# The experts' gate and up projections in f16 halves with a power of two per expert, in a decoder layer with 32 experts

## The chip, the cores and the metric

One core of one Trainium2 chip runs the whole layer in one launch. The metric is the device time of that launch in microseconds, smaller is better. TensorE (PE) multiplies, VectorE (DVE) and ScalarE (ACT) do elementwise work, GpSimd (POOL) gathers and scatters rows, SyncE (SP) issues the large loads. "Block" below means 128 rows of tokens that belong to one expert.

## What is computed

```python
h <- h + W_out[ norm(attention(n(h))) ++ norm(conv(n(h))) ]   # "mixer", 4096 tokens, width 1024
h <- h + HierMoE(n(h))                                        # top-1 group of 4, then top-2 of its 8 experts

def expert_block(args):          # tokens sorted by expert, blocks of 128 rows
    xb, e = args                 # xb 128 x 1024, w_g[e] and w_u[e] 1024 x 512, w_d[e] 512 x 1024
    return (jax.nn.silu(xb @ w_g[e]) * (xb @ w_u[e])) @ w_d[e]
y = ybuf[dest] * gate_s          # weighted by the router's gate and summed per token
```

All inputs are f32. The products have to be nearly f32 exact, so each operand is split into a high and a low half and three products are summed: hi·hi, hi·lo and lo·hi.

## The kernel before

**Two stages.** `mixer` (L211) computes attention, convolution, output projection and routing for 32 tiles of 128 tokens; its projections multiply f16 halves (L574). It ends by writing for every expert a list of its tokens, and a table `blocks_of` with each expert's number of blocks and its first block (L1507 to L1520). `experts` (L1535) then walks through the experts and their blocks; each engine runs its own copy of that walk (`walk`, L1564), and the engines meet in semaphores only.

**One block on PE** (`block_`, L1704): 24 matmuls of 512 columns into psA (gate: 8 slices of the contraction, 3 products each), 4 transposes of the previous block's activation into psE (`turn_act`), 24 matmuls into psB (up), 8 transposes of the next block's gathered rows into psC and psD (`transpose_rows`), and 24 matmuls into psF and psG that are the down projection of the previous block. All these operands (`gT_hi`, `gT_lo`, `aT_hi`, `aT_lo` and the weights' halves) are in the 4-byte format float32r.

**The weights of an expert**: three loads of 2 MB each by SP into the raw buffers `raw["gate"]`, `raw["up"]`, `raw["down"]`, one buffer each (`load_expert`, L168; issued in `sync`, L1587, in the fixed order gate, up, down). SP issues the next expert's load as soon as the present one has been split: ACT copies 512 columns at a time into `hi` (L1770), DVE subtracts that from the raw weights into `lo` (L1812), eight slices each. There is one set of halves, so the split of a new expert begins when the last block of the old one no longer needs them (`gate_ps`, `up_ps`, `y_ps`); PE waits slice by slice (L1673).

**ACT's order in a block** (`halves`, L1734, with L1772 to L1797): in an expert's first block the gate split, `copy_y` (result rows out of psF), in the first block the up split, `turn` (psE into `aT_hi`), `silu` (psA into `gated`), `turn_x` (psC and psD into `gT_hi` for the next block, L1796), and in the first block the down split. DVE follows the same order with the low halves, the product of up and gated (L1826) and its half of the rows (L1819). PE's next block begins when both halves of `gT` are there.

**POOL** loads a block's list of tokens (`slots`, L1632), gathers its rows (L1600), copies row numbers (L1609) and scatters finished rows with an add (L1612).

Of the kernel before, what the change touches and what calls it, by code (L numbers as in the profile page):

```python
# [24 lines left out]
ALU = mybir.AluOpType  # L25
# [9 lines left out]
P = 128  # L35
# [103 lines left out]
def build(nc, x, meta_tokens, rel_bias, mix_norm_g, w_in, q_norm_g, k_norm_g, attn_sinks, conv_w,  # L139
# [12 lines left out]
    with ExitStack() as keep:  # L152
# [24 lines left out]
        rows_of_y = ksb("rows_of_y", [P, 1], I32)  # L177

# [32 lines left out]
def mixer(nc, ctx, env):  # L211
# [3 lines left out]
     cst, ident, blocks_of, held, wi_all, load_expert, raw, keep) = (env[n] for n in (  # L215
         "x2 meta_tokens rel_bias mix_norm_g w_in q_norm_g k_norm_g attn_sinks conv_w attn_out_norm_g "
         "conv_out_norm_g w_out ffn_norm_g w_group_router b_group_router w_expert_router b_expert_router "
         "consts onehot out table hn_dram u_dram band_dram bcast cst ident blocks_of held wi_all load_expert raw keep").split())
# [14 lines left out]
    rt_stat = sb("rt_stat", [P, 8])  # L233
# [71 lines left out]
    hn_scale, inv_rt = rt_stat[:, 4:5], rt_stat[:, 7:8]  # L305
# [58 lines left out]
    planned = 18  # L364
# [711 lines left out]
    def vector(dve):  # L1076
# [60 lines left out]
        def scales_of_router():  # L1137
# [19 lines left out]
            set_up(v.tensor_scalar(inv_rt.bitcast(I32), sI[:, 3:4], float(-(9 << 23)), None, ALU.add))  # L1157
            set_up(v.tensor_scalar(inv_rt, inv_rt, rt_stat[:, 6:7], None, ALU.mult))
# [351 lines left out]
        step(v.tensor_scalar(blocks_of[:, counts], blocks_of[:, E:], 1, None, ALU.max))  # L1510
        step(v.tensor_scalar(blocks_of[:, 0:1], blocks_of[:, 0:1], 2, None, ALU.max))
# [23 lines left out]
def experts(nc, ctx, env):  # L1535
    out, table, hn_dram, cst, ident, blocks_of, held, raw, raw_in, load_expert, keep, mixed = (env[n] for n in (
        "out table hn_dram cst ident blocks_of held raw raw_in load_expert keep mixed").split())
    slots, slots_old, rows_of_y = (env[n] for n in ("slots", "slots_old", "rows_of_y"))
# [8 lines left out]
    hi = {n: sb(f"{n}_hi", [P, 8, 512], F32R) for n in raw}  # L1547
    lo = {n: sb(f"{n}_lo", [P, 8, 512], F32R) for n in raw}
# [4 lines left out]
    y = sb("y", [P, D])  # L1553

    hi_s = {n: sem(f"hi_s_{n}") for n in raw}
    lo_s = {n: sem(f"lo_s_{n}") for n in raw}
    slots_in, moved, shifted, rows_in = sem("slots_in"), sem("moved"), sem("shifted"), sem("rows_in")
# [4 lines left out]
    named = sem("named")  # L1562

    def walk(eng, block, before=None):  # L1564


        def loads(e):
            n = eng.value_load(blocks_of[0:1, bass.ds(e, 1)], min_val=1, max_val=TILES)
            base = eng.value_load(blocks_of[0:1, bass.ds(e + E, 1)], min_val=0, max_val=3 * TILES)
            return n, base  # L1570

        n, _ = loads(0)
        block(0, 0, 0, True)
        block(0, 1, 1, False)
        with eng.If(n > 2):
            with eng.Fori(2, n) as i:
                block(0, i, i, False)
        with eng.Fori(1, E) as e:
            n, base = loads(e)
            block(e, 0, base, True)  # L1580
            with eng.If(n > 1):
                with eng.Fori(1, n) as i:
                    block(e, i, base + i, False)
        n, base = loads(E - 1)
        return base + n

    def sync(sp):  # L1587
        mixed(sp)

        with sp.Fori(1, E) as e:  # L1590
            for n in raw:
                sp.wait_ge(hi_s[n], 8 * e)
                sp.wait_ge(lo_s[n], 8 * e)
                load_expert(sp, n, e)

    def gpsimd(pool):
# [27 lines left out]
        def block_(e, i, b, first):  # L1624
# [13 lines left out]
            if known:  # L1638
# [8 lines left out]
            if known and b == 1:  # L1647
                pool.wait_ge(added, 32)


# [17 lines left out]
    def tensor(pe):  # L1668
        def split_mm(ps, l_k, left, right, r_k, fresh, name=None, e=0):

            for n, k in enumerate(l_k):
                if fresh:
                    pe.wait_ge(hi_s[name], e * 8 + r_k[n] + 1)  # L1673
                    pe.wait_ge(lo_s[name], e * 8 + r_k[n] + 1)
# [19 lines left out]
        def down(b):  # L1694
# [5 lines left out]
            for half, ps in enumerate((psF, psG)):  # L1700
                split_mm(ps, range(KE), (aT_hi, aT_lo), (hi["down"], lo["down"]), [2 * k + half for k in range(KE)],
                         False).then_inc(y_ps, 1)
# [170 lines left out]
```

## Time and profile before

| | us |
|---|---|
| median of 3 runs | 2752.85 (2752.47 to 2755.39) |
| the profiled execution | 2750.93 |
| its span in the trace | 2749.3 |
| mixer and hand-over, up to the first expert matmul | 1329.8 |
| experts, from there to the end | 1419.5 |
| PE busy | 2643.6 (96% of the span) |
| DVE busy, ACT busy | 1716.2, 1391.3 |
| mean granted clock of TensorE | 0.987 of 2.4 GHz |

A time at the start of a row is measured from the start of the span. The profiled execution has 1.6 us outside its span. Durations are per instruction; on PE, ACT and DVE the next instruction starts a little before the former one's duration is over, so the distance of starts is shorter than the duration.

### The profile page before, as it was taken

The numbers are of one execution on the slowest core, as the hardware profiler recorded it, in microseconds if no ns is written. First come the engines' busy times: TensorE is split into PE (matmuls) and PEld (weight loads), VectorE is DVE, ScalarE is ACT, GpSimd is POOL, SyncE is SP. The second block draws the span as 40 slices with busy tenths as digits, with TensorE's granted clock in tenths as the row PEclk, the third lists the DMA queues.
The fourth block names the chain that finished last, engine by engine and source line by source line (L and its number), as shares of the span: only waits on it lengthen the run. The fifth ranks groups of instructions, "written<-read, shape, count | busy, mean of one in ns | idle before, by whom it ended". The sixth has DMA issues, their size and how long they took to land.

```text
span 2749.3 us, 49924 instructions
## 1 busy us (share of the span) xinstructions
PE 2643.6 (96%) x14252; PEld 1820.9 (66%) x14253; DVE 1716.2 (62%) x3920; ACT 1391.3 (51%) x3046; POOL 798.8 (29%) x825
## 2 busy tenths in 40 slices
PE   4999999999999999996699999999999999999997
PEld 2455555555555555553588888888888888888886
DVE  5677777777777777776454455545655444546633
ACT  7666555565555566553344445445545333435533
POOL 1122323232322222331232333323223323333232
PEclk9999999999999999998799999999999999999999
DMA  8376555556655555656556677667767665667763
GB/s 315 82 166 166 156 160 158 152 157 165 163 152 160 154 156 164 166 138 167 187 169 189 186 236 244 200 196 224 235 186 232 205 183 153 194 180 237 235 181 54
DMA packets 546395, 495.22 MB, mean 180 GB/s; under 512 B 411787, under 2 KB 411948, under 8 KB 545340
## 3 DMA queue, kind: packets, MB, share of 16 engines
q1 hardware_dynamic: 517516, 406.08, 49.2%
q0 software_dynamic: 28848, 88.77, 13.8%
q8 instruction: 14, 0.23, 0.0%
q14 instruction: 17, 0.14, 0.0%
HBM read 309.74 MB, written 87.88 MB: 145 GB/s over the span
## 4 chain that ended last, share of the span: by engine, by line
PE 89%; DVE 3%; DMA 3%; ACT 2%; issue 1%; SPq 1%; POOL 1%; POOLq 0%; DVEq 0%; ACTq 0%
PE psB L1676 15%; PE psA L1676 15%; PE psG L574 11%; PE psF L1676 7%; PE psG L1676 7%; PE psE L574 6%; PE psF L574 6%; PE psD L574 6%; PE psC L574 6%; PE psH L574 3%; PE psC L1684 1%; PE psD L1684 1%; PE psE L1691 1%; DMA xg<-hn_rows,slots 1%; DMA slots<-slot_table 1%
## 5 line engine op out<-in xcount | busy, mean ns | idle before, releaser
L574 PE MATMUL psG<-wi_all,both_xT 128*128 128x512 f16 x1536 | 345.2, 382 | 10.9 <-DMA both_xT<-x 10.9
L574 PEld LDWEIGHTS psG<-wi_all,both_xT 128*128 128x128 f16 x1536 | 148.7, 98 | 188.2 <-DMA both_xT<-x 11.1
L1600 POOL DMA_INDIRECT xg<-hn_rows,slots x80 | 99.2, 1240 | 544.0 <-DMA slots<-slot_table 389.4
L1676 PE MATMUL psB<-up_hi,gT_hi 128*128 128x512 f32 x632 | 254.4, 402 | 0.0
L1676 PE MATMUL psA<-gate_hi,gT_hi 128*128 128x512 f32 x632 | 247.3, 391 | 3.1 <-ACT gT_hi L1796 1.7
L1812 DVE TENSOR_TENSOR down_lo<-wi_all,down_hi 128x512 fp32r<-128x512 f32 x256 | 157.0, 686 | 147.1 <-ACT down_hi L1770 147.1
L1676 PE MATMUL psB<-up_hi,gT_lo 128*128 128x512 f32 x632 | 247.6, 392 | 0.0
L1676 PE MATMUL psA<-gate_hi,gT_lo 128*128 128x512 f32 x632 | 247.3, 391 | 0.0
L1676 PE MATMUL psA<-gate_lo,gT_hi 128*128 128x512 f32 x632 | 247.0, 391 | 0.0
L1676 PE MATMUL psB<-up_lo,gT_hi 128*128 128x512 f32 x632 | 246.4, 390 | 0.0
L1796 ACT ACTIVATE gT_hi<-psC 128x512 fp32r<-128x512 f32 x80 | 47.8, 597 | 384.8 <-PE psC L1684 384.8
L1826 DVE TENSOR_TENSOR act_rows<-psB,gated 128x512 f32<-128x512 f32 x79 | 54.6, 691 | 289.6 <-PE psB L1676 289.6
L1770 ACT ACTIVATE down_hi<-wi_all 128x512 fp32r<-128x512 f32 x256 | 137.0, 618 | 149.1 <-PE psG L1676 149.1
L819 ACT ACTIVATE prob<-prob,soft,s_stat 128x256 f32<-128x256 f32 x256 | 150.6, 589 | 94.2 <-DVE soft L1206 94.1
L1609 POOL COPY rows_of_y<-slots 128x1 int32<-128x1 int32 x80 | 129.3, 1616 | 236.9 <-DVE y L1819 236.2
L1812 DVE TENSOR_TENSOR gate_lo<-wi_all,gate_hi 128x512 fp32r<-128x512 f32 x256 | 157.0, 686 | 46.2 <-ACT gate_hi L1770 46.2
L574 PE MATMUL psE<-wo_all,both_mT 128*128 128x512 f16 x768 | 178.5, 383 | 5.9 <-DMA both_mT<-prob 5.9
L574 PE MATMUL psC<-wi_all,both_xT 128*128 128x512 f16 x792 | 178.6, 381 | 4.5 <-DVE wi_all L1186 4.5
L574 PE MATMUL psD<-wi_all,both_xT 128*128 128x512 f16 x792 | 178.2, 380 | 0.0
L574 PE MATMUL psF<-wo_all,both_mT 128*128 128x512 f16 x768 | 176.2, 379 | 0.0
L1770 ACT ACTIVATE gate_hi<-wi_all 128x512 fp32r<-128x512 f32 x256 | 137.0, 618 | 44.5 <-issue 44.5
L1812 DVE TENSOR_TENSOR up_lo<-wi_all,up_hi 128x512 fp32r<-128x512 f32 x256 | 156.7, 685 | 1.0 <-ACT up_hi L1770 1.0
(320 smaller groups left out, 5777.2 us busy)
## 6 DMA issues: line engine op xcount, KB each, us to landing
wi_all<-in_w_gate SPq DMA_DIRECT2D x32, 2048.0 KB, 9.5
wi_all<-in_w_up SPq DMA_DIRECT2D x32, 2048.0 KB, 12.9
wi_all<-in_w_down SPq DMA_DIRECT2D x32, 2048.0 KB, 11.7
xt<-in_x SPq DMA_DIRECT2D x32, 512.0 KB, 3.7
um<-u_rows SPq DMA_DIRECT2D x64, 256.0 KB, 2.7
out_rows<-h SPq DMA_DIRECT2D x32, 512.0 KB, 3.0
xres<-in_x SPq DMA_DIRECT2D x31, 512.0 KB, 4.1
hn_rows<-xres SPq DMA_DIRECT2D x31, 512.0 KB, 2.9
```

The costliest lines, as they stand in the source:

```text
L574: m = nc.tensor.matmul(ps, left[:, l, k, :], weights.half(r, k, n, width), start=(k == opens and j == 0), stop=(k == closes and j == 2))
L819: s.activation(prob[:, hd, :], prob[:, hd, :], ACT.Exp, bias=ntop[:, hd:hd + 1], scale=inv_s, accum_out=psum_[:, hd:hd + 1]).then_inc(p_sb ...
L1600: pool.indirect_dma_start(xg[:], None, hn_dram, bass.IndirectOffsetOnAxis(ap=slots[:, 0, 0:1], axis=0), bounds_check=SEQ + P - 1).then_inc ...
L1609: g.tensor_copy(rows_of_y[:], slots[:, 3, 0:1]).then_inc(named, 1)
L1676: m = nc.tensor.matmul(ps[:, :], l[:, k, :], r[:, r_k[n], :], start=(n == 0 and j == 0), stop=(n == len(l_k) - 1 and j == 2))
L1684: m = nc.tensor.transpose(ps[:, c * P:(c + 1) * P], xg[:, (4 * h + c) * P:(4 * h + c + 1) * P], ident)
L1691: m = nc.tensor.transpose(psE[:, c * P:(c + 1) * P], act_rows[:, c * P:(c + 1) * P], ident)
L1770: s.activation(hi[n][:, k, :], raw[n][:, k, :], ACT.Copy).then_inc(hi_s[n], 1)
L1796: s.activation(gT_hi[:, 4 * h:4 * h + 4, :].rearrange("p k c -> p (k c)"), ps[:, :], ACT.Copy).then_inc(xgT_hi, 1)
L1812: v.tensor_tensor(lo[n][:, k, :], raw[n][:, k, :], hi[n][:, k, :].bitcast(F32), ALU.subtract).then_inc(lo_s[n], 1)
L1826: v.tensor_tensor(act_rows[:], psB[:, :], gated[:], ALU.mult).then_inc(act_s, 1)
```

## The change

Gate and up are split into f16 halves instead of float32r ones. f16 has a short range of exponents, so each expert's gate and up weights are first multiplied by a power of two. To find it, ACT sums the absolute values of the raw weights over each partition (`ACT.Abs` over 4096 columns with `accum_out`), POOL takes the maximum over the partitions (`partition_all_reduce`), and DVE makes the power and its inverse in five small steps (`scales`). The inverses go into `silu`'s scale and into the product. The rows (`gT`) are scaled by the power `hn_scale` that the router has used already. Down keeps its format and its one set. The halves of gate and up exist twice (`p` is 0 or 1): an expert's gate and up are summed in the first block of the expert before it and split in the second. So each expert takes at least two blocks, and the walk handles the experts in pairs. A split is two chunks of 2048 columns instead of eight of 512.

```diff
-        step(v.tensor_scalar(blocks_of[:, counts], blocks_of[:, E:], 1, None, ALU.max))
-        step(v.tensor_scalar(blocks_of[:, 0:1], blocks_of[:, 0:1], 2, None, ALU.max))
+        step(v.tensor_scalar(blocks_of[:, counts], blocks_of[:, E:], 2, None, ALU.max))
...
-    hi = {n: sb(f"{n}_hi", [P, 8, 512], F32R) for n in raw}
+    hi = {n: [sb(f"{n}_hi_{p}", [P, 8, 512], F16) for p in range(2)] for n in SCALED}
+    hi["down"], lo["down"] = ([sb(f"down_{w}", [P, 8, 512], F32R)] * 2 for w in ("hi", "lo"))
-    gT_hi, gT_lo = sb("gT_hi", [P, KD, P], F32R), sb("gT_lo", [P, KD, P], F32R)
+    gT_hi, gT_lo = sb("gT_hi", [P, KD, P], F16), sb("gT_lo", [P, KD, P], F16)
...
         with sp.Fori(1, E) as e:
             for n in raw:
-                sp.wait_ge(hi_s[n], 8 * e)
-                sp.wait_ge(lo_s[n], 8 * e)
+                sp.wait_ge(hi_s[n], CHUNKS * e)
+                sp.wait_ge(lo_s[n], CHUNKS * e)
                 load_expert(sp, n, e)
...
+        def bound_of(e, p):
+            pool.wait_ge(summed, 2 * (e + 1))
+            hold(pool, held)
+            pool.partition_all_reduce(most(p), sums(p), P, RMAX).then_inc(most_s, 1)
...
+        def sum_up(n, e, p, junk):
             act.wait_ge(raw_in[n], 16 * (e + 1))
+            s.activation(junk, raw[n].rearrange("p k n -> p (k n)"), ACT.Abs, accum_out=sums(p, n)).then_inc(summed, 1)
...
+        def block_(e, i, b, p, last):                                  # on ACT
+            if not (known and b < 2):
+                copy_y(b)
+            if first and not last:
+                sum_next("gate", e, p, b)
+            if not (known and b == 0):
+                turn(b)
+            silu(b, p)
+            if first and not last:
+                sum_next("up", e, p, b)
+            if second and not last:
+                split("gate", e + 1, 1 - p)
+            turn_x(b + 1)
+            if first:
+                split_down(e, b)
+            if second and not last:
+                split("up", e + 1, 1 - p)
```

**ACT, the first block of an expert.** Before, from the loop over the experts (`gate_hi`, `up_hi`, `down_hi` are the splits, `y` is `copy_y`, `gT_hi` is `turn_x`):

```order
L1770 ACTIVATE gate_hi<-wi_all 128x512 [waits raw_in_gate]
L1770 ACTIVATE gate_hi<-wi_all 128x512 x7
...
L1777 ACTIVATE y<-psF,slots 128x512 [waits added]
L1770 ACTIVATE up_hi<-wi_all 128x512 [waits raw_in_up,up_ps]
L1770 ACTIVATE up_hi<-wi_all 128x512 x7
...
L1789 ACTIVATE aT_hi<-psE 128x512 [waits y_ps]
...
L1783 ACTIVATE gated<-psA 128x512 [waits act_s,gate_ps]
...
L1796 ACTIVATE gT_hi<-psC 128x512 [waits xgT_ps]
...
L1796 ACTIVATE gT_hi<-psD 128x512 [waits xgT_ps]
...
L1770 ACTIVATE down_hi<-wi_all 128x512 [waits raw_in_down,y_ps]
L1770 ACTIVATE down_hi<-wi_all 128x512 x7
```

Now, where `gate_hi,own` and `up_hi,own` are the sums of the next expert's raw weights:

```order
L1797 ACTIVATE y<-psF,slots 128x512 [waits added]
...
L1771 ACTIVATE gate_hi,own<-wi_all 128x4096 [waits raw_in_gate]
...
L1809 ACTIVATE aT_hi<-psE 128x512 [waits y_ps]
...
L1803 ACTIVATE gated<-psA,own 128x512 [waits act_s,gate_ps]
L1771 ACTIVATE up_hi,own<-wi_all 128x4096 [waits raw_in_up,up_ps]
...
L1816 ACTIVATE gT_hi<-psC,rt_stat 128x512 [waits xgT_ps]
...
L1816 ACTIVATE gT_hi<-psD,rt_stat 128x512 [waits xgT_ps]
...
L1790 ACTIVATE down_hi<-wi_all 128x2048 [waits y_ps]
L1790 ACTIVATE down_hi<-wi_all 128x2048
```

The splits of gate and up have left this block, and two instructions that wait for the next expert's loads stand ahead of `gT_hi`.

**DVE, the second block of an expert, now** (with the down split's low halves ahead of it, which are issued in the first block):

```order
L1885 TENSOR_TENSOR down_lo<-wi_all,down_hi 128x2048 [waits hi_s_down] x2
...
L1892 TENSOR_SCALAR y<-psG,slots 128x512 [waits added]
...
L1868 TENSOR_SCALAR own<-own 128x2 [waits most_s]
...
L1872 TENSOR_SCALAR own<-own,rt_stat 128x2 [waits step_s]
...
L1904 TENSOR_TENSOR aT_lo<-psE,aT_hi 128x512 [waits step_s,aT_hi_s]
...
L1879 SCALAR_TENSOR_TENSOR gate_lo<-wi_all,own,gate_hi 128x2048 [waits hi_s_gate]
...
L1879 SCALAR_TENSOR_TENSOR gate_lo<-wi_all,own,gate_hi 128x2048 [waits hi_s_gate]
L1900 SCALAR_TENSOR_TENSOR act_rows<-psB,own,gated 128x512 [waits aT_ps,up_ps,silu_s]
...
L1911 SCALAR_TENSOR_TENSOR gT_lo<-psC,rt_stat,gT_hi 128x512 [waits xgT_hi]
...
L1911 SCALAR_TENSOR_TENSOR gT_lo<-psD,rt_stat,gT_hi 128x512 [waits xgT_hi]
L1879 SCALAR_TENSOR_TENSOR up_lo<-wi_all,own,up_hi 128x2048 [waits hi_s_up] x2
```

The low halves of the next expert's gate and up come after the whole of the present expert's down split, and only when the last `up_lo` is done is the raw buffer of up free for another load. SP's own order (gate, up, down) is unchanged.

## Rows read from the trace of the kernel before

**Rows 1.** The page: the chain that ended last, by engine.

```profile
PE 89%; DVE 3%; DMA 3%; ACT 2%; issue 1%; SPq 1%; POOL 1%; POOLq 0%; DVEq 0%; ACTq 0%
```

**Rows 2.** The chain of waits through one block: start us, us, what.

```profile
1434.76 5.44 PE psA L1676 x24
1440.20 0.44 PE psE L1691 x4
1440.64 5.49 PE psB L1676 x24
...
1452.46 5.44 PE psA L1676 x24
```

**Rows 3.** Groups by line on PE, experts: shapes, count | busy us, mean ns.

```profile
L1676 PE MATMUL psA<-gate_hi,gT_hi 128*128 128x512 f32 x632 | 247.3, 391 | 3.1 <-ACT gT_hi L1796 1.7 <-DVE gT_lo L1836 1.5
```

**Rows 4.** The chain of waits in the mixer: f16 matmuls of 512 columns.

```profile
1207.71 5.18 PE psD L574 x24
```

**Rows 5.** Timeline of SP's queue: start us, us, engine, line, what.

```profile
1437.40 0.37 SPq L172 DMA_DIRECT2D wi_all<-in_w_gate  x1
...
1490.52 0.37 SPq L172 DMA_DIRECT2D wi_all<-in_w_gate  x1
...
1525.94 0.37 SPq L172 DMA_DIRECT2D wi_all<-in_w_gate  x1
```

**Rows 6.** ACT by form: scaled and long activations, accumulator read; busy us, mean ns.

```profile
L861 ACT ACTIVATE a<-xres,rt_stat 128x1024 f16<-128x1024 f32 x29 | 33.3, 1148 | 42.1 <-DVE xres L1288 42.1
L803 ACT ACTIVATE wi_all<-wi_all,g_mix 128x1280 f16<-128x1280 f32 x8 | 10.9, 1362 | 5.2 <-DVE wi_all L1186 2.7 <-DVE g_mix L1176 2.5
L791 ACT ACTIVATE wi_all<-wi_all 128x2304 bf16<-128x2304 f32 x8 | 17.0, 2122 | 4.7 <-DMA wi_all<-in_w_in 4.7
L773 ACT ACTIVATION_READ_ACCUMULATOR x<-xt 128x1 f32 x33 | 6.2, 187 | 0.0
```

**Rows 7.** DVE by form: two widths of the instruction that makes f16 halves; `copy_y`.

```profile
L1186 DVE SCALAR_TENSOR_TENSOR wi_all<-wi_all,g_mix 128x1024 f16<-128x1024 f32 x8 | 10.2, 1279 | 0.0
L1186 DVE SCALAR_TENSOR_TENSOR wi_all<-wi_all,g_mix 128x1280 f16<-128x1280 f32 x8 | 12.4, 1552 | 3.1 <-ACT wi_all L803 3.1
L1819 DVE TENSOR_SCALAR y<-psG,slots 128x512 f32<-128x512 f32 x79 | 58.9, 746 | 76.5 <-PE psG L1676 41.7 <-DMA out_rows<-y,rows_of_y 34.8
```

**Rows 8.** Timeline of DVE: two small steps, one waiting for the other.

```profile
1310.69 0.18 DVE L1509 TENSOR_SCALAR blocks_of<-blocks_of 128x32 int32<-128x32 int32 x1
1310.91 0.18 DVE L1510 TENSOR_SCALAR blocks_of<-blocks_of 128x32 int32<-128x32 int32 x1
```

**Rows 9.** Timelines of ACT, DVE and PE at the first expert block.

```profile
1328.40 0.60 ACT L1796 ACTIVATE gT_hi<-psD 128x512 fp32r<-128x512 f32 x1 [0.26 <-PE psD L1684]
1329.03 0.69 DVE L1836 TENSOR_TENSOR gT_lo<-psD,gT_hi 128x512 fp32r<-128x512 f32 x1 [0.16 <-ACT gT_hi L1796]
1329.82 0.77 PE L1676 MATMUL psA<-gate_hi,gT_hi 128*128 128x512 f32 x1 [1.46 <-DVE gT_lo L1836]
```

**Rows 10.** Landing of the 32 up loads (view of the tensor in_w_up).

```profile
DMA to landing us min/median/max: 9.9/12.9/14.0
```

**Rows 11.** POOL by line: the maximum over the partitions.

```profile
L1004 POOL PARTITION_ALL_REDUCE scale_w<-scale_w x2 | 0.7, 365 | 29.7 <-DVE scale_w L1169 29.7
```

**Rows 12.** The chain of waits at the first two expert blocks.

```profile
1329.82 8.12 PE psA L1676 x24
1345.94 5.73 PE psA L1676 x24
```

**Rows 13.** Timeline of PE around a gap in the mixer.

```profile
1275.64 5.04 PE L574 MATMUL psE<-wo_all,both_mT 128*128 128x512 f16 x12 [5.86 <-DMA both_mT<-prob]
1280.52 2.75 PE L574 MATMUL psF<-wo_all,both_mT 128*128 128x512 f16 x12
```

**Rows 14.** Windows in two gaps of PE; last three columns: granted clock, DMA share, GB/s.

```profile
1274.00:1275.60 1.60, 0.00 (x0) 0.00 (x0) 1.06 (x2) 1.57 (x3) 0.00 (x0) 0.50 0.43 108
1289.00:1294.00 5.00, 0.00 (x0) 0.00 (x0) 1.94 (x3) 2.79 (x5) 0.00 (x0) 1.00 0.41 167
1295.00:1299.00 4.00, 0.00 (x0) 0.00 (x0) 3.41 (x18) 0.39 (x2) 0.00 (x0) 0.50 0.78 186
```

**Rows 15.** POOL's copy of row numbers behind a series of splits on DVE (timeline).

```profile
1438.14 4.55 POOL L1609 COPY rows_of_y<-slots 128x1 int32<-128x1 int32 x1 [6.86 <-DVE y L1819]
```

More of the change, by code:

```diff
@@ L363, in mixer @@
     last = sig("last").sem
-    planned = 18
+    planned = 17
     LAST = TILES
@@ L1562, in experts, with walk, expert @@
     named = sem("named")
[L1564 to L1585, printed above, removed]
+    SCALE_STEPS = 5
+    def walk(eng, block):
+        def expert(e, p, last=False):
+            n = eng.value_load(blocks_of[0:1, bass.ds(e, 1)], min_val=2, max_val=TILES)
+            base = eng.value_load(blocks_of[0:1, bass.ds(e + E, 1)], min_val=0, max_val=4 * TILES)
+            start = 0 if isinstance(e, int) and e == 0 else base
+            block(e, 0, start, p, last)
+            block(e, 1, start + 1, p, last)
+            with eng.If(n > 2):
+                with eng.Fori(2, n) as i:
+                    block(e, i, start + i, p, last)
+            return base + n
+        expert(0, 0)
+        with eng.Fori(0, (E - 2) // 2) as pair:
+            expert(pair * 2 + 1, 1)
+            expert(pair * 2 + 2, 0)
+        return expert(E - 1, 1, True)
     def sync(sp):
@@ L1637, in block_ @@
             gather()
-            if known:
+            if known and b < 2:
                 pool.wait_ge(cleared, 3)
@@ L1648, in block_ @@
                 pool.wait_ge(added, 32)
+            if isinstance(i, int) and i == 1 and not last:
+                bound_of(e + 1, 1 - p)
+        bound_of(0, 0)
         mixed(pool)
@@ L1700, in down, with weights, block_ @@
             for half, ps in enumerate((psF, psG)):
-                split_mm(ps, range(KE), (aT_hi, aT_lo), (hi["down"], lo["down"]), [2 * k + half for k in range(KE)],
-                         False).then_inc(y_ps, 1)
-        def block_(e, i, b, first):
+                split_mm(ps, range(KE), (aT_hi, aT_lo), (hi["down"][0], lo["down"][0]),
+                         [2 * k + half for k in range(KE)]).then_inc(y_ps, 1)
+        def weights(n, e):
+            pe.wait_ge(hi_s[n], CHUNKS * (e + 1))
+            pe.wait_ge(lo_s[n], CHUNKS * (e + 1))
+        def block_(e, i, b, p, last):
             static0 = isinstance(b, int) and b == 0
+            first, second = isinstance(i, int) and i == 0, isinstance(i, int) and i == 1
             pe.wait_ge(xgT_hi, 2 * (b + 1))
@@ L1782, in silu @@
                 act.wait_ge(act_s, b)
-            s.activation(gated[:], psA[:, :], ACT.Silu).then_inc(silu_s, 1)
+            s.activation(gated[:], psA[:, :], ACT.Silu, scale=inverse(p, "gate")).then_inc(silu_s, 1)
         def turn(b):
@@ L1845, in vector @@
         dve.sem_inc(y_dve, 3)
-        halves(dve, split, copy_y, product, turn, turn_x)
+        split("gate", 0, 0)
+        turn_x(0)
+        split("up", 0, 0)
+        total = walk(dve, block_)
+        copy_y(total)
+        turn(total)
+        copy_y(total + 1)
     return dict(sync=sync, tensor=tensor, scalar=scalar, gpsimd=gpsimd, vector=vector)
```

175 lines of the change are left out of this document (112 added, 63 removed).

## The prediction, made before the changed kernel was run

> **What bounds the kernel now.** I read the page's chain that ended last first, then the chain of waits in the expert stage, then the timelines of the engines that feed PE. The chain is PE for 89% [rows 1]. In the expert stage one block follows another with no gap: 24 gate matmuls take 5.44 us, 24 up matmuls 5.49, and the next block begins 17.70 us after the last (1452.46 - 1434.76) [rows 2]. The group of one of the three gate products counts 632 matmuls; at 8 a block that is 79 blocks [rows 3]. An expert's length is the distance of two gate loads on SP's queue: 53.12 us is three blocks, 35.42 is two [rows 5]. Of the 30 distances that the trace has, 16 are of two blocks (35.1 to 35.9) and 14 of three; none is of one, so raising the smallest count to two adds no block. The 16 lie in 6 runs of neighbours. So anything that shortens a matmul shortens the kernel, and any lateness of what PE waits for, `gT_hi` and `gT_lo` above all, lengthens it.
>
> **Faster matmuls.** 24 f16 matmuls of 512 columns take 5.18 us in the mixer [rows 4], against 5.44 and 5.49 here [rows 2]. I take 5.18 for gate and 5.23 for up, which starts behind transposes as now: 0.26 twice, 0.52 us a block, times 79 = **-41 us**. The bounds are nothing (the step to f16 brings no pace) and this.
>
> **The new wait.** What the order of ACT shows is that in an expert's first block two sums stand ahead of `gT_hi`, and each waits for a load of the next expert. The load of up cannot be issued before the split of up into the other set is over, a block earlier, because raw weights have one buffer. I follow one turn for a run of two-block experts, with time 0 at the start of the gate matmuls of a second block.
>
> - ACT is free 0.9 us before that: `gT_hi` starts 1.42 before PE does and holds ACT for 0.5 [rows 9]. It splits down in chunks of 2048 columns. 1148 ns at 1024 columns and 1362 at 1280 make 0.84 ns a column, so 2.0 us, or 1.9 from start to start [rows 6]. First chunk done at 1.0.
> - DVE's chunk: 1279 and 1552 ns make 1.07 ns a column, 2.37 us at 2048, 2.3 from start to start [rows 7]. Two chunks of down: 5.6. `copy_y` 0.7 [rows 7]: 6.3. Five steps of `scales`, 0.22 each with its wait [rows 8], and a little for the extra semaphore counts: 7.6.
> - ACT's first chunk of gate: 9.5. DVE's two: 14.1. Product and `gT_lo`: 16.0. Two chunks of up: 20.6. SP then issues the load of up, at 21.0.
> - It lands 9.9 to 14.0 us later, 12.9 in the median [rows 10]. I take 12.9, since a load of gate and a scatter run ahead of and beside it as now: 33.9.
> - The sum: 2122 ns at 2304 columns and 0.84 ns for each of 1792 more, and 187 for the accumulator [rows 6], 3.8 us: 37.7. Then both `gT_hi` and the last `gT_lo`, 0.5 and 1.4 [rows 9]: PE can go on at 39.6.
>
> PE's own work up to there is two blocks, 2 x 17.18 = 34.4. It waits **5.2 us**. In the first expert of a run the block before was on time; then the split of down starts with the end of PE's down matmuls at 0, not at -0.9, and the wait is 6.1. An expert of three blocks gives the chain 17.2 us more and no wait follows. So 10 x 5.2 + 6 x 6.1 = **+89 us**. With a landing of 9.9 the waits are 2.2 and 3.1, together 41; with 14.0 they are 6.3 and 7.2, together 106.
>
> Part of the wait will show one stage earlier: the sum of gate, whose load lands late as well, stands ahead of `aT_hi`, so the down matmuls of the first block will begin a microsecond or two late. This is inside the 5.2, not beside it.
>
> **The start.** Expert 0's up split starts on ACT at about 1329.0 [rows 9]; 1.9 and 4.6 later its raw buffer is free, the load is issued at 1335.9 and, with nothing beside it, lands in 9.9: 1345.8. Plus 3.8 and 1.9 is 1351.5. Block 1 begins at 1345.94 now [rows 12]: **+6 us**. The first sums, of expert 0, lie in the idle time at the end of the mixer.
>
> **The clock.** A gap of 5.86 us in the mixer ended with the granted clock at 0.50, which is 1.2 GHz, and 12 matmuls then took 5.04 us where the next 12 started 2.59 apart in sum (2.75 long) [rows 13, 14]. In another gap the clock was still 1.00 five microseconds in, and 0.50 after six [rows 14]. The new gaps are of this size, partly cut in two. One drop costs about 2.4 us; but the chain above is not PE's, so in a run PE's slowness mostly shortens the next wait. I take a drop in a third of the 17 gaps, half of it felt: with the start's, **+5 us**. Bounds: 0 and 17 x 2.4 = 41. The Trainium skill ("TensorE: Matmul & The Clock Gate", "Why this matters for your kernels") says that pauses between bursts of matmuls let the clock fall back each time. By that rule taken whole the sum would be at the upper bound. The trace agrees for the 5.86 us gap, and shows one gap that held full clock for five.
>
> **At no cost.** The maximum over partitions is 0.4 us [rows 11] and is asked for some 8 us before DVE uses it. But POOL stands in that wait until 37.7, and behind it are the list and the rows of the second block; a fetch and a gather need some 7 us, the transposes come 11.3 after 39.6, so 4 to 5 us of cover are left. If the fetch lies behind a scatter, the cover goes and up to 3 us a wait are added. POOL's small copies can be held up by DVE's splits (4.55 us once per expert now [rows 15]); chunks leave this as it is. Fewer instructions on ACT and DVE save nothing, since neither was waited for. The extra copy and the one step less in the mixer's tail cancel.
>
> **Sum**: -41 + 89 + 6 + 5 = +59. The profiled execution is 2750.9, so 2810; the median of the runs is 1.9 higher, so **2812 us**.
>
> **Rivals.**
> - *The waits are hidden.* If the chain from one second block to the next takes less than 34.4 us, nothing is left but the shorter matmuls: 2752.85 - 41 = 2712 us. For it: two sets of halves, and splits that begin a block ahead. Against it: up would have to land within 7.7 us of its issue, below the fastest of 32. This is the faster side. 0.06.
> - *Loads land early.* With the load of up alone in the queue it may take 9.9: 41 + 6 - 41 = +6, so 2759, and 2770 if waits lie between. 0.12.
> - *The clock falls in every gap.* The sum with 41 in place of 5: 2848. By the skill's rule above this would be the likeliest; the held gap speaks against it, and that a slow PE eats its own wait. 0.14.
> - *f16 brings no pace to PE* (the change does not do what it is for): the wait falls to 4.2 each, since a block stays at 17.70: 73 + 6 + 5 = 2837. Against it: the mixer's f16 matmuls run at 5.18 in the same program. 0.04.
> - The forecast as worked out: 0.60. The rest, 0.04, is a mix of several or a cost unseen.
>
> **Range.** The forecast's own range follows from the landing, 10.5 to 14 us, and the clock: 2775 to 2845. Early loads and the clock rival are taken in down to 2772 and up to 2850. About 0.2% is what a measurement of this kernel can tell from no change, 5.5 us; faster by more 0.07, within 0.05, slower by more 0.88.
>
> **What would show it right.** The 24 gate matmuls at 5.18 us. ACT idle before the Abs on raw up, released by the DMA of up, and PE idle before psA of an expert's second block for about 5 us, released by `gT_hi` or `gT_lo`, 16 or 17 times; no such idle time after an expert of three blocks. SP's up load some 6.4 us behind gate's, and gate loads of a two-block expert about 39.6 us apart. It is wrong if PE's idle time lies elsewhere (POOL's rows, the weights' own waits), if PE has no idle time, or if matmuls keep 5.44.

## The result, and the profile after

The changed kernel takes 2846.3 us, the median of 4 runs (2842.2 to 2849.9), against 2753.1 us (2752.5 to 2755.4): a ratio of 1.034, 95% interval 1.032 to 1.036. The forecast was 2812, with a range of 2772 to 2850. So the sign and the range held, the range by 4 us, and 34 us were missing from the sum.

| | before | after |
|---|---|---|
| span of the profiled execution | 2749.3 us | 2843.3 us |
| mean granted clock | 0.987 | 0.974 |
| first gate matmul of the experts | 1329.82 | 1335.17 |
| second block begins | 1345.94 | 1357.12 |
| block with no wait in it | 17.70 us | 17.16 us |

The page of the kernel after, busy time by engine, and the chain that ended last:

```profile
PE 2635.8 (93%) x14252; PEld 1485.7 (52%) x14253; DVE 1725.0 (61%) x3504; ACT 1597.3 (56%) x2598; POOL 722.7 (25%) x857
...
PE 73%; DMA 12%; issue 5%; DVE 4%; ACT 3%; SPq 1%; POOL 1%; POOLq 1%; DVEq 0%; ACTq 0%
```

PE had 89% of the chain [rows 1] and now has 73%; DMA went from 3% to 12%. What took PE's place is seen in the chain of waits around the first long wait of the experts (start us, us, what):

```profile
1546.05 2.73 PE psG L1703 x12
1548.78 0.03 issue
...
1551.48 0.19 ACT up_hi L1771
1551.66 1.16 ACT gT_hi L1816 x2
1552.83 1.07 issue
1553.90 7.25 PE psA L1703 x24
1561.15 0.44 PE psE L1718 x4
```

PE is done with an expert's first block at 1548.78 and cannot go on until ACT has read out the sum of up (the row of 0.19) and made `gT_hi`. The gap is 5.1 us. The chain calls the last 1.07 us "issue"; the timeline shows what they are, the low halves of the rows on DVE:

```profile
1553.06 0.74 DVE L1911 SCALAR_TENSOR_TENSOR gT_lo<-psD,rt_stat,gT_hi 128x512 f16<-128x512 f32 x1
1553.90 0.59 PE L1703 MATMUL psA<-gate_hi,gT_hi 128*128 128x512 f16 x1 [5.13 <-issue]
```

The 24 gate matmuls behind the gap take 7.25 us, not 5.18. The windows before the gap, in it and over these matmuls show the clock (the last three columns are granted clock, DMA share, GB/s):

```profile
1531.40:1548.70 17.30, 17.25 (x84) 10.43 (x84) 6.37 (x5) 6.19 (x6) 3.67 (x3) 1.00 0.92 303
1548.80:1553.80 5.00, 0.00 (x0) 0.00 (x0) 1.41 (x2) 5.00 (x5) 0.90 (x4) 0.72 0.00 0
1553.90:1561.10 7.20, 7.20 (x25) 2.95 (x26) 5.86 (x8) 3.09 (x3) 1.76 (x3) 0.73 0.31 84
```

ACT itself waited for the loads. From its timeline, the two sums in an expert's first block further on:

```profile
1672.76 3.62 ACT L1771 ACTIVATE gate_hi<-wi_all 128x4096 bf16<-128x4096 f32 x1 [5.10 <-DMA wi_all<-in_w_gate]
...
1684.06 3.62 ACT L1771 ACTIVATE up_hi<-wi_all 128x4096 bf16<-128x4096 f32 x1 [6.53 <-DMA wi_all<-in_w_up]
1687.59 0.18 ACT L1771 ACTIVATION_READ_ACCUMULATOR up_hi<-wi_all 128x1 f32 x1
1687.68 0.67 ACT L1816 ACTIVATE gT_hi<-psC,rt_stat 128x512 f16<-128x512 f32 x1
```

The loads issued ahead of these two sums left SP's queue at 1664.28 and 1670.70. The list of waits gives the whole of it (in total us, times, longest us):

```profile
POOL own L1650 <- ACT up_hi L1771: 302.7, 31, 13.7
...
ACT up_hi L1771 <- DMA wi_all<-in_w_up: 100.9, 17, 7.8
...
ACT gate_hi L1771 <- DMA wi_all<-in_w_gate: 79.6, 17, 6.4
...
PE psA L1703 <- issue: 66.7, 31, 6.4
```

So far this is the forecast. What it did not have is in the chain of waits from the second of these sums on, up to the next load of up:

```profile
1687.59 0.19 ACT up_hi L1771
...
1688.00 0.18 POOL own L1650
...
1690.82 2.06 DMA slots<-slot_table
...
1693.89 9.73 DMA xg<-hn_rows,slots
...
1703.66 0.67 PE psC L1711 x4
...
1705.51 2.01 ACT up_hi L1783
...
1712.41 12.20 DMA wi_all<-in_w_up
```

The chain runs from the sum of up over POOL's bound, the fetch of the list and **the gather of the rows** to PE's transposes, then to the split of up, and to the next load of up. The two up loads, 1670.70 and 1712.41, are 41.7 us apart. The gather takes 9.73 us; in the kernel before its median was 4.5. SP issued the load of down at 1695.38, 1.5 us after the gather. The gather is what made the rows late here: PE had finished the 24 up matmuls at 1702.6 and needed the rows then; with 4.5 us they would have been there at 1698.4 (an estimate from these rows).

A table of the start of every group of matmuls in PE's timeline, all 79 blocks, adds up as follows. Each part is the time above that of an undisturbed block.

| part | us | blocks |
|---|---|---|
| start: first gate matmul 5.35 later, block 1 another 5.83 later | +11.2 | |
| 78 blocks, each 0.54 shorter | -42.1 | |
| waits before the gate matmuls, long | +57.7 | 15 |
| the same, 0.40 to 0.63 us each | +7.5 | 15 |
| waits before the transposes: rows are late | +32.7 | 19 |
| gate matmuls at the lower clock | +24.0 | 12 |
| down matmuls at the lower clock, behind the two longest waits before the transposes (3.1 and 3.2 us) | +3.2 | 2 |
| sum (the spans differ by 94.0) | +94.2 | |

### The profile page after: what moved, and what is told of

Read it like the earlier page. It is cut to its first block, busy times and chain, and to the rows that moved or that the text cites. A ratio compares the mean times of both kernels' runs of the same rounds, so it can differ in the third digit from the quotient of the medians.

```text
span 2843.3 us, 48164 instructions
## 1 busy us (share of the span) xinstructions
PE 2635.8 (93%) x14252; PEld 1485.7 (52%) x14253; DVE 1725.0 (61%) x3504; ACT 1597.3 (56%) x2598; POOL 722.7 (25%) x857
## 4 chain that ended last, share of the span: by engine, by line
PE 73%; DMA 12%; issue 5%; DVE 4%; ACT 3%; SPq 1%; POOL 1%; POOLq 1%; DVEq 0%; ACTq 0%
PE psG L575 11%; PE psA L1703 10%; PE psB L1703 9%; DMA xg<-hn_rows,slots 6%; PE psF L1703 6%; PE psG L1703 6%; PE psE L575 6%; PE psF L575 5%; PE psD L575 5%; PE psC L575 5%; PE psH L575 3%; DMA wi_all<-in_w_up 3%; DMA slots<-slot_table 2%; PE psC L1711 1%; PE psD L1711 1%
## 5 line engine op out<-in xcount | busy, mean ns | idle before, releaser
L575 PE MATMUL psG<-wi_all,both_xT 128*128 128x512 f16 x1536 | 345.2, 382 | 11.3 <-DMA both_xT<-x 11.2
L1703 PE MATMUL psA<-gate_hi,gT_hi 128*128 128x512 f16 x632 | 250.6, 396 | 68.4 <-issue 66.7
L1703 PE MATMUL psA<-gate_lo,gT_hi 128*128 128x512 f16 x632 | 250.2, 396 | 0.0
L1703 PE MATMUL psA<-gate_hi,gT_lo 128*128 128x512 f16 x632 | 249.5, 395 | 0.0
L1703 PE MATMUL psB<-up_lo,gT_hi 128*128 128x512 f16 x632 | 239.5, 379 | 0.0
L1703 PE MATMUL psB<-up_hi,gT_hi 128*128 128x512 f16 x632 | 239.5, 379 | 0.0
L1703 PE MATMUL psB<-up_hi,gT_lo 128*128 128x512 f16 x632 | 239.5, 379 | 0.0
L1885 DVE TENSOR_TENSOR down_lo<-wi_all,down_hi 128x2048 fp32r<-128x2048 f32 x64 | 143.8, 2288 | 99.9 <-ACT down_hi L1790 99.9
L1879 DVE SCALAR_TENSOR_TENSOR gate_lo<-wi_all,own,gate_hi 128x2048 f16<-128x2048 f32 x64 | 147.7, 2348 | 47.4 <-ACT gate_hi L1783 47.4
L1771 ACT ACTIVATE up_hi<-wi_all 128x4096 bf16<-128x4096 f32 x31 | 112.1, 3617 | 100.9 <-DMA wi_all<-in_w_up 100.9
L1790 ACT ACTIVATE down_hi<-wi_all 128x2048 fp32r<-128x2048 f32 x64 | 118.6, 1903 | 70.9 <-PE psG L1703 70.9
## 6 DMA issues: line engine op xcount, KB each, us to landing
wi_all<-in_w_up SPq DMA_DIRECT2D x32, 2048.0 KB, 12.8
wi_all<-in_w_down SPq DMA_DIRECT2D x32, 2048.0 KB, 11.2
```

The lines of the kernel that those rows point to most:

```text
L575: m = nc.tensor.matmul(ps, left[:, l, k, :], weights.half(r, k, n, width), start=(k == opens and j == 0), stop=(k == closes and j == 2))
L1703: m = nc.tensor.matmul(ps[:, :], l[:, k, :], r[:, r_k[n], :], start=(n == 0 and j == 0), stop=(n == len(l_k) - 1 and j == 2))
L1771: s.activation(junk, raw[n].rearrange("p k n -> p (k n)"), ACT.Abs, accum_out=sums(p, n)).then_inc(summed, 1)
L1790: s.activation(chunk(hi["down"][0], c), chunk(raw["down"], c), ACT.Copy).then_inc(hi_s["down"], 1)
L1879: v.scalar_tensor_tensor(chunk(lo[n][p], c), chunk(raw[n], c), power(p, n), chunk(hi[n][p], c), ALU.mult, ALU.subtract).then_inc(lo_s[n], 1)
L1885: v.tensor_tensor(chunk(lo["down"][0], c), chunk(raw["down"], c), chunk(hi["down"][0], c).bitcast(F32), ALU.subtract).then_inc(lo_s["down" ...
```

## The experiments

Each was run with rounds of the kernel before on the same chip; the ratios are to that.

**No sums.** `sum_next` and POOL's `bound_of` for the next expert are left out; all experts use the power of expert 0:

```diff
-            if isinstance(i, int) and i == 1 and not last:
-                bound_of(e + 1, 1 - p)
...
-                sum_next("gate", e, p, b)
...
-                sum_next("up", e, p, b)
```

> The changed kernel without the next expert's sums (ACT), without their maximum (POOL) and without the steps for the powers after expert 0, whose powers serve all experts; two sets, pairs, f16 and the order of all else stay. Load theory (PE waits because the sums stand ahead of gT_hi and of POOL's next list, and their loads land late): all waits for gT and for rows go, 2753 - 41 + 7 for the change of expert, and perhaps 5 at the start, so 2715 to 2727 us. Rival (the pairs, the two sets or the two-block split themselves cost it): stays above 2790 us.

Measured: 2772.7 us, ratio 1.008 (1.006 to 1.009), between the two. All waits before the gate matmuls were gone, and the time was 74 us less than the change's. But in 29 blocks PE now stood before the transposes, 47.4 us in all, though POOL waited for no sum. Neither theory had that.

**Two raw buffers** for gate and up, each loaded a whole expert ahead, sums and bounds in place:

```diff
+        raw = {n: [r, r] for n, r in raw.items()}
+            raw[n][1] = wi_flat[:, 12288 + j * 4096:12288 + (j + 1) * 4096].rearrange("p (k n) -> p k n", k=8)
...
+                for n in SCALED:
+                    free(n, pair * 2 + 1 + d, pair * 2 + 2 + d, d)
```

> The changed kernel with a second raw buffer for gate and for up, so that the next but one expert's loads are issued once the same buffer was split, 17 us or more earlier, ahead of the down load; all sums, maxima and steps stay. Load theory: the sums find their weights there, no wait for gT or rows: 2753 - 41 + 7 + 11 at the start = about 2730 us. Rival (ACT or POOL has too much work in the first block, whatever the loads do): 2790 us or more, with e1 fast.

Measured: 2748.8 us, ratio 0.9986 (0.9976 to 0.9995). The list of waits has no more wait of ACT for a load of gate or up, and no wait before the gate matmuls was longer than 0.7 us. The sums took as long as ever, so the late loads, not the 3.8 us that a sum takes, are the bulk of the 94 us. The waits before the transposes fell as well, from 32.7 to 5.7 us: this edit gives time to both loops at once. What remained over the expectation: a start 12.5 us later than before, and 30 gaps of 0.42 to 0.68 us.

**Sum of up behind `gT_hi`** in ACT's order:

```diff
             silu(b, p)
-            if first and not last:
-                sum_next("up", e, p, b)
...
             turn_x(b + 1)
+            if first and not last:
+                sum_next("up", e, p, b)
```

> The changed kernel with one line moved: on ACT the sum of up comes after gT_hi instead of ahead of it. If the place ahead of gT_hi is all of the cost: about 2735 us. Load theory: the turn of one raw buffer (split down, scales, split gate and up, load, sum) is still some 38 us long against PE's 34.4, and POOL's list for the second block still waits for the sum, so rows come late and about half of the loss stays: 2790 to 2825 us, with the idle time of PE now ahead of the transposes of xg and of the down matmuls.

Measured: 2948.2 us, ratio 1.071 (1.069 to 1.073). A miss, and the most telling one. The chain of waits of this kernel, over one expert:

```profile
1650.30 12.89 DMA wi_all<-in_w_up
...
1667.21 0.17 POOL own L1650
...
1669.09 2.09 POOL slots_old L1639
...
1671.33 2.05 POOL slots L1642
...
1674.16 5.21 DMA slots<-slot_table
...
1680.38 11.15 DMA xg<-hn_rows,slots
...
1691.58 1.11 PE psC L1711 x4
...
1694.43 1.73 ACT up_hi L1783
```

The wait did not go, it moved: POOL's bound still holds back the list and the rows until the sum is made. PE waited 173.7 us before the transposes in 29 blocks, up to 14.7 us at once, and the matmuls behind these waits, at the lower clock, took some 53 us more. There are two loops through the load of up, one over `gT_hi` and one over the rows. Opening the first lengthened the second: POOL's two copies take 2.1 us each here, not 0.2, the list's fetch 5.2 and the gather 11.2. Why the copies are slow was not tested.

**Half the sum** (only the first 2048 of 4096 columns are summed, so the bound covers half of the weights):

```diff
-            s.activation(junk, raw[n].rearrange("p k n -> p (k n)"), ACT.Abs, accum_out=sums(p, n)).then_inc(summed, 1)
+            s.activation(junk[:, 0:2048], raw[n][:, 0:4, :].rearrange("p k n -> p (k n)"), ACT.Abs, accum_out=sums(p, n)).then_inc(summed, 1)
```

> The changed kernel with each sum over the first 2048 of 4096 columns, so the other half of the weights is not looked at. The sum of up is on the chain, so each two-block expert gets shorter by 1.7 us (3.61 to about 1.9): 16 x 1.7 and as much at the start = 29, so 2846 - 29 = about 2817 us. If the sum is not on the chain (the loss lies in rows, code or clock): 2840 to 2850 us.

Measured: 2822.7 us, ratio 1.026 (1.024 to 1.028): 23.6 us less for a sum that is 1.7 us shorter, some 15 times. The sum of up is on the chain. In the traces the waits before the gate matmuls fell by 21 us and those before the transposes rose by 5, so the waits alone give 16, two thirds of the full length; 6 more came from fewer matmuls at the lower clock. At the start nothing was gained: block 1 began 0.25 us earlier.

**Plain f16.** The kernel before, with f16 halves of gate, up and rows, one constant power of two for all experts (`WS` = 256), and nothing else of the change:

```diff
-    hi = {n: sb(f"{n}_hi", [P, 8, 512], F32R) for n in raw}
+    hi = {n: sb(f"{n}_hi", [P, 8, 512], F32R if n == "down" else F16) for n in raw}
...
-                s.activation(hi[n][:, k, :], raw[n][:, k, :], ACT.Copy).then_inc(hi_s[n], 1)
+                    s.activation(hi[n][:, k, :], raw[n][:, k, :], ACT.Copy, scale=WS).then_inc(hi_s[n], 1)
```

> The kernel before, with its order, its eight slices for each split, its one set of halves and its one raw buffer; only gate, up and the transposed rows are split into f16 halves, and all experts share one constant power of two (256) in place of each expert's own, so no sum and no bound is computed. If the whole loss of the change comes from the sums, the late loads and POOL's bound, and f16 alone is worth 0.52 us for each of 79 blocks, this takes 2752.9 - 41 = 2712 us (2706 to 2722), with 24 gate matmuls at 5.18 to 5.19 us and blocks 17.16 us apart. Rival: the splits that follow PE slice by slice have too little time beside the faster matmuls, and PE waits for a slice at each expert; then 2725 to 2752.

Measured: 2718.9 us, ratio 0.987 (0.985 to 0.988). Blocks follow each other at 17.16 us. 8 blocks wait for rows, 10.7 us in all, and the first gate matmul came at 1334.81, 5.0 us later than before, though this kernel has neither sum nor bound. Of these 5.0 us, 3.8 lie ahead of the experts: POOL writes the last list at 1316.17, before at 1312.38. Why the mixer ends later here, these runs do not tell.

**Spread loads.** The kernel without sums, with the split of gate in an expert's first block:

```diff
-            if second and not last:
+            if first and not last:
                 split("gate", e + 1, 1 - p)
```

> As the kernel without sums and bound (all experts share one constant power of two, 2772.7 us), but ACT and DVE split gate of the next expert in the first block of an expert in place of the second, at the same point of the block. There the three loads of an expert were issued within 13.5 us (down, 7.1 us later gate, 6.4 us later up) and the gathered rows came last: PE waited before the transposes in 29 blocks, 47 us in all. Here the loads are issued about 10 to 12 us apart. If the bunched loads are what held up the rows, the waits before the transposes go and the time is 2772.7 - 47 - 5 = 2721 us (2712 to 2732). Rival: rows are late because of POOL's own queue (its copies beside DVE's long chunks); then nothing changes, 2765 to 2775.

Measured: 2718.8 us, ratio 0.987 (0.986 to 0.989); the waits before the transposes fell from 47.4 to 0.7 us. The same instructions in another order gave 54 us, though the loads did not spread as expected: down and gate went out 1 us apart, up 12 us later. So the time is as expected, but not by the loads' being spread evenly.

**Two raw buffers, early power.** DVE's five steps move to the end of the first block:

```diff
-            if second and not last:
-                scales(e + 1, 1 - p)
...
             if first:
+                if not last:
+                    scales(e + 1, 1 - p)
                 split_down(e)
```

> The change with two raw buffers for gate and up (2748.8 us), and DVE's five steps that make the power moved from the second block of an expert to the end of its first, ahead of the split of down. With two raw buffers PE still stood 0.42 to 0.63 us before the gate matmuls in 30 blocks, 16 us in all: in the second block ACT's split of gate began only when the power was ready, and pushed gT_hi, and DVE's gT_lo, past PE. If that is so, the 16 us go: 2733 us (2729 to 2738). Rival: the two chunks of DVE's gate split (4.6 us) are what pushes gT_lo whatever their start; then 2745 to 2750.

Measured: 2779.0 us, ratio 1.009 (1.008 to 1.010): outside both. The 30 small gaps had gone, as the theory says, and 46 us of waits for rows had come in 29 blocks.

**Sums without a bound.** The kernel without sums, with ACT's two sums put back, which nobody uses; all experts use the power of expert 0:

```diff
+            if first and not last:
+                sum_next("gate", e, p, b)
...
+            if first and not last:
+                sum_next("up", e, p, b)
```

> The change with both of ACT's sums of the next expert in their places, but nothing uses them: all experts share one constant power of two, and POOL doesn't wait for the sums nor run the maximum over partitions. This separates ACT's part from POOL's. If POOL's stand in that wait is what makes the rows late, the 33 us of waits before the transposes (19 blocks) fall to less than 8 and the 58 us of waits before the gate matmuls, with up to 24 us of slower matmuls behind them, stay: 2846 - 28 = 2818 us (2808 to 2826). If the rows are late because of the weight loads in front of them, the waits before the transposes stay too: 2840 to 2850. If POOL's hold is what makes everything late, the time falls to near 2772, that of the kernel without sums.

Measured: 2839.6 us, ratio 1.032 (1.030 to 1.033), between the first two cases, at the edge of the second. Waits before the transposes fell to 20.8 us in 13 blocks, every one of them with a weight load issued within 1.6 us of its gather, but the long waits before the gate matmuls grew to 61.9 in 16 and the slow gate matmuls to 30 us in 15. So POOL's stand is worth 7 us of the 94, and the loop over ACT's sum and `gT_hi` gives nearly the whole loss alone. The loop over the rows alone (the sum of up behind `gT_hi`) gave twice the loss.

**Two raw buffers, up and gate together.**

```diff
-                for n in SCALED:
+                for n in ("up", "gate"):
```

> The kernel with two raw buffers and the early power (2779.0 us), with one line changed: SP waits for the raw buffer of up before that of gate, so the loads of an expert go out as up, at once gate, and 18 us later down, in place of down, 7.1 us later gate and 6.4 us later up. There the gap before the gate matmuls had gone as expected, but the rows came late in 29 blocks (46 us of waits before the transposes, 6 before down, and slower matmuls behind some). If the bunch of three loads ahead of the gathered rows is the cause, all of that goes and what is left over the kernel before is the start (the second block 15.3 us later) and what is gained the shorter matmuls (42 us): 2753 + 15 - 42 = 2726 us (2721 to 2736). Rival: it is the early power that makes the rows late, by DVE's five steps ahead of the split of down or by what follows from them; then 2765 to 2785. Second rival: gate and up side by side are enough to hold the rows up; then 2740 to 2765.

Measured: 2764.6 us, ratio 1.004 (1.003 to 1.005), on the border of the two rivals, and 39 us over the theory: 29 blocks waited for rows, 37.3 us. Setting down 18 us apart from the other two does not bring the rows in time. The timelines of SP's queue and of POOL, this kernel:

```profile
1666.34 0.37 SPq L175 DMA_DIRECT2D wi_all<-in_w_up  x1
1666.88 0.46 SPq L175 DMA_DIRECT2D wi_all<-in_w_gate  x1
```

```profile
1665.58 1.48 POOL L1635 DMA_INDIRECT xg<-hn_rows,slots  x1 [4.56 <-ACT y L1810]
...
1675.14 0.36 POOL L1663 PARTITION_ALL_REDUCE own<-own  x1 [5.31 <-DMA xg<-hn_rows,slots]
```

The loads go out within the same microsecond as the gather, which lands some 9 us after its issue. I then went through the gathers of all traces with SP's loads beside them, and counted the blocks that waited over 0.3 us for their rows. "Beside" is a load issued within 1.75 us of the gather's start, before or after; the limit was chosen with the traces in sight. The first two gathers are left out. "Landing" is the median from the start of a gather with a load beside it until its rows were there (with a star: where the trace doesn't record it, until the transposes, over the blocks that waited), and "PE ready" the median time from the same start until PE had nothing left to do ahead of the transposes:

| kernel | load beside: blocks that waited | others | landing, us | PE ready, us |
|---|---|---|---|---|
| before | 0 of 11 | 0 of 67 | 9.3 | 9.5 |
| after | 19 of 23 | 0 of 55 | 9.6* | 7.9 |
| no sums | 27 of 27 | 2 of 51 | 8.5* | 7.1 |
| two raw buffers | 2 of 2 | 0 of 76 | 9.4* | 6.5 |
| sum of up behind `gT_hi` | 18 of 33 | 11 of 45 | 9.9* | 7.9 |
| half the sum | 18 of 23 | 1 of 55 | 9.6* | 8.2 |
| plain f16 | 8 of 10 | 0 of 68 | 9.3* | 8.2 |
| spread loads | 0 of 29 | 1 of 49 | 7.1 | 7.7 |
| two raw buffers, early power | 27 of 27 | 2 of 51 | 8.4 | 7.0 |
| sums without a bound | 13 of 20 | 0 of 58 | 8.4 | 7.1 |
| two raw buffers, up and gate together | 28 of 28 | 1 of 50 | 9.8 | 9.0 |

Without a load beside it a gather lands in 4.4 to 4.5 us in the median. With one it takes 7.1 to 9.9, and PE waits where it is ready before that; in the kernel before, and with the loads spread, it is not. The kernel with the sum of up behind `gT_hi` is apart, since there the gathers themselves start late. The kernel before had shown the price already, in the list of its transfers (KB each, median us to landing) and in the view of the tensor `xg`:

```profile
xg<-hn_rows,slots POOLq DMA_INDIRECT x80, 4.5
slots<-slot_table POOLq DMA_DIRECT2D x79, 1.0 KB, 6.3
```

```profile
DMA to landing us min/median/max: 4.2/4.5/9.8
```

With the loads spread, only up's 2 MB leave within 12 us ahead of the gather, and it takes 7.1.

**Two raw buffers, up last.** The same kernel with the order gate, down, up on SP's queue, which puts no load beside the gather:

```diff
-                for n in SCALED:
-                    free(n, pair * 2 + 1 + d, pair * 2 + 2 + d, d)
+                free("gate", pair * 2 + 1 + d, pair * 2 + 2 + d, d)
                 free("down", pair * 2 + 1 + d, pair * 2 + 1 + d)
+                free("up", pair * 2 + 1 + d, pair * 2 + 2 + d, d)
```

> The kernel with two raw buffers and the early power (2779.0 us), SP's order of loads gate, down, up in place of gate, up, down: up now goes out beside down, 6.8 us into the second block, instead of 0.4 us ahead of the gathered rows (there the gather was issued at 1672.65, the load of up at 1672.2, and the rows landed 8.9 us later; the fastest gather needs 4.2). If it is a load issued at the same moment as the gather that holds the rows up, not how close the three loads are, the waits before the transposes go: 2779 - 46 - 6 = 2727 us (2722 to 2738). Rival: 4 MB at once beside the next fetch of the list move the gather itself, and rows stay late: 2750 to 2785.

Measured: 2732.6 us, ratio 0.993 (0.991 to 0.995), as expected. SP's queue, POOL, and the landing of all gathers in the expert stage, this kernel:

```profile
1676.70 0.37 SPq L175 DMA_DIRECT2D wi_all<-in_w_down  x1
1677.22 0.40 SPq L175 DMA_DIRECT2D wi_all<-in_w_up  x1
1683.84 0.37 SPq L175 DMA_DIRECT2D wi_all<-in_w_gate  x1
```

```profile
1690.85 1.07 POOL L1635 DMA_INDIRECT xg<-hn_rows,slots  x1 [5.85 <-DVE y L1905]
...
1698.39 0.36 POOL L1663 PARTITION_ALL_REDUCE own<-own  x1 [3.71 <-DMA xg<-hn_rows,slots]
```

```profile
DMA to landing us min/median/max: 4.1/4.5/8.3
```

Gate now leads the gather by 7.0 us, up by 13.6; from the third gather on none has a load within 1.75 us, and 4 of 78 made PE wait over 0.3 us. Here the gather still takes over 7 us, but no longer 9; the median of all is 4.5, and the waits for rows are down to some 6 us. This version keeps each expert's own power of two and all of the change's arithmetic, and beats both kernels: 20 us under before, 114 under the change.

**Two raw buffers, product between the chunks.** DVE puts `product` and `gT_lo` between its two chunks of gate's split:

```diff
-                split("gate", e + 1, 1 - p)
+                split("gate", e + 1, 1 - p, [0])
             product(b, p)
             turn_x(b + 1)
+            if second and not last:
+                split("gate", e + 1, 1 - p, [1])
```

> The kernel with two raw buffers (2748.8 us) with the power made where the change makes it, but DVE puts the product and gT_lo between its two chunks of gate's split. If the 16 us of gaps before the gate matmuls come from DVE's 4.6 us of gate split ahead of gT_lo, they go. The gate raw buffer then comes free some 2.6 us later, and gate's load goes out within a microsecond of the gather of the next rows; by the theory that a load issued beside the gather holds it up by 4 to 5 us, the rows come 0 to 1 us late in most of 30 blocks. Gain 16, loss 0 to 30: 2733 to 2763, most likely 2745 us. Rival (a load beside the gather costs nothing): 2733 us.

Measured: 2747.0 us, ratio 0.998 (0.997 to 1.000). The gaps went from 16.1 us in 30 blocks to 7.5 in 16, the waits for rows from 5.7 to 10.9. Gate's load left 1 to 3 us ahead of the gather, as expected, but up's left 4.4 us later in place of 6.4. 25 gathers had a load within 1.75 us and took 8.7 us in the median; PE was ready 9.2 us after their start, and only 6 blocks waited for rows. The price of a load beside the gather is there, but PE pays it only past its slack. The gain is not to be told from none against the kernel with two raw buffers.

## Why the prediction was right, and by what it fell short

- **Faster matmuls**, -41 forecast, -42 measured: 5.19 and 5.18 us for 24, a block 17.16. The plain f16 kernel has it alone.
- **The wait behind the sum of up**, +89 forecast. The mechanism, the place and its terms held: up's load 6.4 us behind gate's; landing 12.8 in the median for 12.9; the sum 3.62 and 0.19 for 3.8; waits in 15 of the 16 experts that follow one of two blocks and in no others, but for gaps of 0.4 to 0.6 us. In the first expert of each of the 6 runs the wait was 5.3 to 6.3, 5.6 in the mean, for 6.1. In the other 9 it was 2.7 in the mean, for 5.2; there the rows had held PE up before. The 17 distances of gate loads over two blocks are 39.0 to 42.8 us, 40.9 in the mean; forecast 39.6. No sums, two raw buffers and half a sum bear out that it is the load of up, and the sum behind it, that these waits come from. Measured: 57.7 + 7.5 before gate and 32.7 before the transposes, together 98. That these come near 89 is in part luck: a third of them is in a place where the forecast had none, which was its own sign of being wrong ("POOL's rows").
- **The step that failed is the one under "At no cost".** It put a fetch and a gather at some 7 us and so gave POOL's hold 4 to 5 us of cover, to be lost only if the fetch lay behind a scatter. The page of the kernel before has the two at 6.3 and 4.5 us in the median, and a gather at 9.8 in the worst case. In the rows above, the bound ends at 1688.2, the gather starts at 1693.9 and lands 9.73 us later: 15.4 us, and PE was ready after 14.5. The cover was gone in 19 blocks, not by a scatter but by weight loads issued beside the gather. So part of the waits is in front of the transposes, and there are two loops of about the same length.
- **The clock**, +5 forecast, 27 measured: 24 in the gate matmuls of 12 blocks, 3 in the down matmuls of two. Of the 15 long waits before gate, three of 1.6 to 2.2 us and one of 3.7 were followed by matmuls at full pace; the other 11, of 2.6 to 6.3 us, by 1.3 to 2.9 us more for 24, and so was the wait before block 1. I had taken a drop in a third of the gaps; that was too few. I had also taken half of each as eaten by the next wait. ACT's timeline speaks against that:

```profile
1697.51 0.60 ACT L1809 ACTIVATE aT_hi<-psE 128x512 fp32r<-128x512 f32 x1 [4.41 <-PE psE L1718]
1698.00 0.68 ACT L1803 ACTIVATE gated<-psA,own 128x512 f32<-128x512 f32 x1
1698.57 3.89 ACT L1783 ACTIVATE gate_hi<-wi_all,own 128x2048 f16<-128x2048 f32 x2
```

  Behind the slow gate matmuls come `aT_hi` and the silu, and only then the split of gate, from which the next loads follow; here ACT had stood 4.41 us for PE. So a slow PE delays its own feeder in this place. How much of the 27 us the next waits ate, no run separates. The Trainium skill ("TensorE: Matmul & The Clock Gate", "Why this matters for your kernels") warns of the longer idle gaps between bursts of matmuls, not of every pause. The trace agrees, and its rule is nearer than my third: 11 of the 12 waits of 2.6 us and more before gate were followed by slow matmuls, and none of the 18 shorter ones.
- **The start**, +6 forecast for block 1, which came 5.83 later against the first block, as worked out. But the first block itself was 5.35 late, for which the forecast had nothing. In this trace 4.03 us of it lie on POOL before the first maximum over partitions of the stage:

```profile
1318.91 0.30 POOLq L1594
1319.52 4.03 issue
1323.55 0.25 POOL own L1650
```

  The last list was written at 1313.56, 1.2 us later than before. The plain f16 kernel was 5.0 late too, but there 3.8 us lie ahead of that point. From that point to the fetch of the first block's list it is 10.2 us here, 6.4 in the kernel before and 6.9 in plain f16. So the 4 us come behind the hand-over, ahead of the maximum; whether the maximum causes them was not tested.

In the sum: -42 for -41, waits 98 for 89, clock 27 for 5, start 11 for 6, which makes 94 for 59. The forecast's own range ended at 2845; 2846.3 lies inside only because the clock rival had been taken in, up to 2850. That rival came nearest in time (2848), and its mechanism was there in 11 of 15 waits; but of the missing 35 us 9 came from the waits and 5 from the start. Hidden waits and early loads are ruled out by the list of waits, f16 without a pace of its own by the 5.18 us.

## What to carry to other kernels

A wait put at the end of a queue that also feeds data (here POOL's bound ahead of the list and the rows) can be on the path as soon as what it waits for comes late, though here it was worth only 7 us: follow the loop from a buffer's release over its load and back through *every* engine that stands in between, and take the longest. If a single raw buffer sits between a load and two readers in different blocks (the sum, then the split), give that a second buffer before anything else. And look at which transfers leave within a microsecond of each other: an edit that only frees an engine a little earlier can put a 2 MB load beside a small gather that PE needs.

## What the runs showed of the hardware

- **A gather of 128 rows beside a 2 MB load**: 4.4 to 4.5 us in the median without one; 9.3 in the kernel before and 7.1 to 9.9 in the other kernels with a load issued within 1.75 us of it. The Trainium skill says ("DMA: Bandwidth & Descriptors", "Issuing engines are not separate DMA queues") that transfers of all engines run on the same 16 DMA engines and interleave; the traces agree, and add the size of it. Five small steps made earlier cost 30 us by this, and another order of three loads gave 46 back.
- **TensorE's clock**, in the changed kernel: 18 gaps of 0.4 to 2.2 us before the gate matmuls left the next 24 at 5.18 us; of 12 gaps of 2.6 to 6.3 us only one, of 3.7 us, did. The border is not sharp: in the kernel without a bound gaps of 3.6 and 4.0 us left the pace whole, in the one with the sum of up behind `gT_hi` waits of 2.2 and 2.4 us before the transposes were followed by 12 down matmuls in 3.7 and 3.8 us, not 2.8. With the granted clock at 0.73 over the 7.2 us behind a gap, part of that time is at 1.2 GHz and part at 2.4.
- **f16 against the 4-byte format** at 512 columns: 5.18 against 5.44 us for 24, and the weight load took 98 ns against 188. The gain per block is the same with each expert's own power and with one constant: 17.16 us between blocks in both.
